# Longer rows for two pairs of on-chip tensors in an fp32r transformer kernel

## What is computed

```
def swiglu(x, w_gate, w_up, w_down):
    return (jax.nn.silu(x @ w_gate) * (x @ w_up)) @ w_down
for l in range(2):
    x = x + 0.5 * swiglu(rmsnorm(x, ffn1_norm[l]), ...)      # 1024 -> 2 x 2816 -> 1024
    p = rmsnorm(x, mix_norm[l]) @ w_in[l]                     # 1024 -> 2048
    x = x + concatenate([y_pool, y_four, y_attn]) @ w_out[l]
    x = x + 0.5 * swiglu(rmsnorm(x, ffn2_norm[l]), ...)
x = rmsnorm(x, final_norm)
for layer in range(2):                                        # second model
    x = x + concatenate([oa * silu(a_g), ob * silu(b_g), om * silu(m_g)]) @ w_out
```

## Time and profile before

| | |
|---|---|
| time of two runs | 2522.74 and 2517.0 us, median 2519.87 us |
| the profiled execution | 2521.43 us, its span 2519.6 us |
| TensorE matmul busy | 2446.2 us (97%), 10934 instructions |
| weight loads busy | 1925.9 us (76%), beside the matmuls |
| VectorE, ScalarE, GpSimd busy | 1133.1, 1082.4, 1120.8 us |
| mean granted TensorE clock | 0.991 of full speed |

### The profile page before, as it was taken

One profiled execution on the slowest core, in us unless ns is written; L12 is line 12 of the kernel. 1 busy time (PEld: TensorE's weight loads), 2 busy tenths in 40 slices (PEclk: granted clock), 3 DMA queues, 4 the chain that ended last, 5 costly groups with the idle time before them and its releaser, 6 DMA issues.

```text
span 2519.6 us, 30096 instructions
## 1 busy us (share of the span) xinstructions
PE 2446.2 (97%) x10934; PEld 1925.9 (76%) x10934; DVE 1133.1 (45%) x1780; ACT 1082.4 (43%) x1584; POOL 1120.8 (44%) x828
## 2 busy tenths in 40 slices
PE   8999999989999999999999989999999998999988
PEld 6888888657888888888888668888887675776666
DVE  5544115564444105544025655444136655465553
ACT  4333224454333214333133544333225777357772
POOL 4544445415555445554445424554445232343333
PEclk9999999999999999999999999999999999999999
DMA  4222223212222222222223203222232222132212
GB/s 169 87 100 100 100 89 128 84 34 101 100 86 97 100 100 91 92 100 100 101 85 132 82 23 113 85 99 100 100 134 94 78 82 65 67 103 69 84 63 84
DMA packets 37528, 233.17 MB, mean 93 GB/s; under 512 B 5184, under 2 KB 5312, under 8 KB 10816
## 3 DMA queue, kind: packets, MB, share of 16 engines
q1 hardware_dynamic: 36000, 226.51, 25.8%
q10 hardware_dynamic: 1440, 5.45, 0.6%
HBM read 223.55 MB, written 2.10 MB: 90 GB/s over the span
## 4 chain that ended last, share of the span: by engine, by line
issue 58%; POOL 41%; POOLq 1%
POOL w_lo L438 41%; POOLq L432 0%; POOLq L436 0%; POOLq L212 0%; POOLq L438 0%; POOLq L1875 0%
## 5 line engine op out<-in xcount | busy, mean ns | idle before, releaser
L438 POOL TENSOR_TENSOR w_lo<-raw,w_hi 128x512 fp32r<-128x512 f32 x824 | 1120.6, 1392 | 1398.3 <-ACT w_hi L925 1398.2
L446 PE MATMUL ps<-h_hi,w_hi 128*128 128x512 f32 x2304 | 921.4, 400 | 14.2 <-DVE h_lo L1331 8.0
L448 PE MATMUL ps<-h_hi,w_lo 128*128 128x512 f32 x2304 | 900.2, 391 | 0.0
L447 PE MATMUL ps<-h_lo,w_hi 128*128 128x512 f32 x2304 | 900.0, 391 | 0.0
L925 ACT ACTIVATE w_hi<-raw 128x1024 fp32r<-128x1024 f32 x412 | 413.2, 1051 | 869.1 <-PE ps L448 865.1
L446 PEld LDWEIGHTS ps<-h_hi,w_hi 128*128 128x128 f32 x2304 | 434.6, 189 | 116.5 <-issue 14.0
L447 PEld LDWEIGHTS ps<-h_lo,w_hi 128*128 128x128 f32 x2304 | 434.6, 189 | 92.8 <-issue 6.0
L448 PEld LDWEIGHTS ps<-h_hi,w_lo 128*128 128x128 f32 x2304 | 434.2, 188 | 92.3
L446 PE MATMUL ps<-hid_hi,w_hi 128*128 128x512 f32 x704 | 273.9, 389 | 0.0
L447 PE MATMUL ps<-hid_lo,w_hi 128*128 128x512 f32 x704 | 273.9, 389 | 0.0
L448 PE MATMUL ps<-hid_hi,w_lo 128*128 128x512 f32 x704 | 273.9, 389 | 0.0
(11 more groups left out here) (236 smaller groups left out, 2085.7 us busy)
## 6 DMA issues: line engine op xcount, KB each, us to landing
raw<-in_stream SPq DMA_DIRECT2D x206, 1024.0 KB, 4.8
hraw<-xs SPq DMA_DIRECT2D x96, 64.0 KB, 2.0
x_sb<-in_x SPq DMA_DIRECT2D x4, 512.0 KB, 10.9
out_x<-x_sb SPq DMA_DIRECT2D x8, 256.0 KB, 2.7
mem_sb<-in_mem ACTq DMA_DIRECT2D x1, 1024.0 KB, 10.7
rec_sb<-in_recip ACTq DMA_DIRECT2D x2, 512.0 KB, 4.3
memn<-in_mem ACTq DMA_DIRECT2D x1, 1024.0 KB, 5.0
dist_sb<-in_dist ACTq DMA_DIRECT2D x2, 448.0 KB, 3.3
```

The source lines that it names most:

```text
L438: gp.tensor_tensor(w_lo[:, s, c], raw[:, s, c], w_hi[:, s, c].bitcast(F32), ALU.subtract).then_inc(lo_split, 1)
L446: pe.matmul(dst, l_hi, r_hi, start=first, stop=False)
L447: pe.matmul(dst, l_hi, r_lo, start=False, stop=False)
L448: return pe.matmul(dst, l_lo, r_hi, start=False, stop=last)
```

## The change

Each row of `hid_hi` and `hid_lo` is allocated with 4 floats (16 bytes) more, and each row of `h_hi` and `h_lo` with 16 floats (64 bytes) more; the slice `[:, :, 0:T]` leaves the added ones unused. 8 floats (32 bytes) are left free between `h_hi` and `h_lo`. `region` grows by 256 floats (1024 bytes) to hold the longer `hid` tensors. No instruction, wait or DMA is added, removed or moved; only addresses differ.

```
-        hid_hi = sb("hid_hi", [P, FB, T], F32R, ffn)
-        hid_lo = sb("hid_lo", [P, FB, T], F32R, ffn)
+        hid_hi = sb("hid_hi", [P, FB, T + 4], F32R, ffn)[:, :, 0:T]
+        hid_lo = sb("hid_lo", [P, FB, T + 4], F32R, ffn)[:, :, 0:T]
...
-        sb("region", [P, 2 * FB * T])
+        sb("region", [P, 2 * FB * T + 256])
         w_hi = sb("w_hi", [P, 2, PANEL], F32R)
         w_lo = sb("w_lo", [P, 2, PANEL], F32R)
-        h_hi = sb("h_hi", [P, KB, T], F32R)
-        h_lo = sb("h_lo", [P, KB, T], F32R)
+        h_hi = sb("h_hi", [P, KB, T + 16], F32R)[:, :, 0:T]
+        sb("h_gap", [P, 8])
+        h_lo = sb("h_lo", [P, KB, T + 16], F32R)[:, :, 0:T]
         x_sb = sb("x_sb", [P, KB, T])
         raw = sb("raw", [P, 2, PANEL])
         cst = sb("cst", [P, NC])
```

## The result

The changed kernel takes 2556.78 us (two runs, 2556.78 and 2556.79) against 2519.87 before: a ratio of 1.0151, 95% interval 1.0129 to 1.0173. It is slower by 37 us, where no change was forecast, and 7 us above the range. The profiled execution has a span of 2555.0 us against 2519.6.

The account below looks back on a forecast made before the run. The kernel was taken as bound by the pitch of its fp32r matmuls on TensorE. Four terms of 0 left the profiled 2521.4 us, put at 2520 us since that execution was 1.6 us above the timed median; range 2495 to 2550.

Parts of the forecast that it names:

- What bounds the kernel: Whole kernel: bound by the 226.6 ns pitch of TensorE's fp32r matmuls, 13.3 ns above their columns; TensorE busy 2446.2 of 2519.6 us.
- Term 1: Pitch of 9216 matmuls with a shifted operand: 13.3 ns surplus held whatever the addresses, so change taken at 0.
- Terms 2, 3 and 4: Panel splitting, VectorE's feed-forward work, writes to `h` at the borders: each taken at 0, the last bounded at 2.2 us.
- The first rival: TensorE's moving-row and weight reads conflict and padding parts them: 2419 us if all but 2 ns goes; chance 0.15.
- The second rival: Matmul rows starting off a 64-byte boundary cost up to 0.01 us more: 2612 us, or 2564 in part; chance 0.10.

Follow-up runs that it names:

- e10: Kernel before the change with 32 bytes left free between `h_hi` and `h_lo` only, row lengths unchanged: 2551.01 us, ratio 1.0122.
- e1: No computation, only chains of 48 fp32r matmuls, one pair of operand offsets each: pitch 226.6 ns with the moving row at 0 bytes, 233.6 at 32.
- e9: Kernel before the change with 64 bytes left free ahead of `h_hi`, row lengths unchanged: 2535.09 us, ratio 1.006.
- mm: Chain in e1 with the moving row alone shifted, to 192 bytes: settled pitch 233.3 ns.
- turned_a: Chain in e1 with the weights alone shifted, to 64 bytes: settled pitch 233.3 ns.
- e11: No computation, only chains of 40 fp32r matmuls with 512 to 412 and 256 to 220 columns, at equal offsets and 32 bytes off: 227.9 ns at 508.

## Why the prediction was wrong

**What bounds the kernel** was right: TensorE's pitch, with no cover. The whole loss stands in the starts of its matmuls. The count of 9216 matmuls held. (The stretch of 320 us holds most of a down stage, up to 1880 of 1889 us, and not all of it; nothing hangs on that.)

**Term 1 failed**, and by it alone the forecast. It took the change of the pitch at 0; measured are 25.8 + 11.2 + 1.4 = 38.4 us on 9216 matmuls, 4.2 ns each. Three inferences in it carried too far.
The bounds of the term, 101 us below and 92 above, held the truth; the choice of the value in the middle didn't, since nothing in the trace was near to it. The range then cut the dear side at 2550 by giving it one chance in twenty. The change did stay within 2%, to which the text gave 0.85, but nearly all of that chance stood on an even pitch.

**Terms 2, 3 and 4** were right. L438, L1405, L1331 and L1337 keep their durations within 8 ns, and the waits for `h_lo` stay at 8.0 and 2.6 us.

**The first rival** named what acts, the relation of the two operands' addresses, and had the wrong sign: it took the equal offsets of before for the conflict and the padding for the cure. Equal offsets are among the best cases at 512 columns (226.7 ns), and padding spreads the rows over the others, whose mean is 231.0. Its remark that row 0 of `h_hi` would keep 227 ns is wrong as well: at 230 to 236 it suffers from its neighbours, as in e10.

**The second rival** had the sign and nearly the size (2564 us), by luck: its reason, own starts off 64 bytes, is refuted by e1 and e9.

**What stays open** is how the relation of the addresses acts. That the reads of moving row and weights meet in the memory fits, since moving either one alone changes the pitch (`mm` and `turned_a` in e1), but no chain ran without a weight load beside its matmuls, which would show whether the surplus and the layout's effect go with it. The effect doesn't grow with the amount of weights read, as fewer weight columns were dearer in e1, and it isn't a whole round of the memory per row, by e11. Why an odd multiple of 16 bytes for the weights has a table of its own, and what picks one of two patterns in the same layout (e9, e10), is open too.

## What to carry to other kernels

Back-to-back fp32r matmuls of 512 columns have a pitch that depends on where their operands lie: 226.7 to 235 ns at multiples of 16 bytes, mostly by the distance of moving row and weights modulo 256 bytes. For 512 columns keep row lengths and tensor starts at multiples of 256 bytes from the weights; for another length measure, as at 256 columns 32 bytes off was cheaper. And look at the difference of addresses when a tensor of odd size is put in front of matmul operands; 32 bytes cost 36 us of 2520 here. A number that never varies in a trace may mean that its cause never varied: ask what values the trace has sampled before calling it a constant, and price the untested ones as unknown.

## What the runs showed that was not expected

The pitches of a chain are not noise: in the changed kernel the pattern of 48 repeats in 77 panels to within 1 ns, while three other engines and the DMAs work beside it. Yet a layout can have more than one such pattern: in e9 one up stage of four settles at 233.3 ns and the rest at 228.9. bf16 (216 ns) and fp32 (429 ns) at full clock are the same at offsets of 0, 16 and 64 bytes, fp32r is not. Fewer columns can take longer (508 at 227.9 ns, 512 at 226.7), and so can fewer weight columns (32 at 231.7 ns, 128 at 226.7). At half the clock this shift costs nothing: in the changed kernel, too, the seven pitches from 2166.36 to 2169.34 us, at a granted clock of 0.50, are 0.426 us each, as in the earlier trace rows.
